# Low parts of the heads' weight tiles: one GpSimd instruction of 1024 columns, or four of 256

## The chip, the cores and the metric

The kernel runs on one core of a Trainium2 chip. A core has five engines that work side by side: TensorE (PE in the profile; PEld is its weight load), VectorE (DVE), ScalarE (ACT), GpSimd (POOL) and SyncE (SP), which issues most transfers. They meet only at semaphores. The metric is device microseconds (us) of the whole program; of several runs the median counts.

## What is computed

One inference step of a decoder layer for 1024 prompt tokens and 8 sample tokens (1032 columns in all), cut to what matters:

```python
xn = rmsnorm(x, p['rms_mix_g']) * (1.0 + sc_m) + sh_m
qa, ka, va, qb, fb, ib, ogb, ga, gb = split_in(xn @ p['w_in'])   # 1024 x (9 * 1024)
oa = attend(rope(rmsnorm(qa)), rope(rmsnorm(ka)), va, lam)       # 8 heads, causal, two softmaxes
ob = recur(silu(qb), 1 - f, log(f), ib)                          # 8 heads, f from sigmoid(fb)
merged = sigmoid(ga) * (oa @ w_branch_a) + sigmoid(gb) * (ob @ w_branch_b)
x = x + g_m * (merged @ p['w_out'])
u = hn @ p['w_up']                                               # then conv, silu(a) * g, @ w_down
```

All of it is in float32.

## The kernel before

**Products in three terms.** Each float32 operand is held as two parts: a high part (`hi`, written by ScalarE in the type fp32r, which TensorE reads) and a low part (`lo` = raw − hi). A product is three matmuls for each of the 8 row blocks `k` of a 1024-row weight tile: hi·hi, hi weights on the low part of x, low weights on the high part of x (`product`, L172). A weight tile is 128x1024: `raw` is loaded by SyncE, `hi` is a ScalarE copy (L780), and `lo` is a subtraction on GpSimd (`lo_of`, L1203), 58 times in the heads stage.

**Stages.** The stages follow one another with a barrier between them: norm (to about 64 us), heads (to about 1092 us), gates, and the tail with the output projections and the feed-forward part. The change lies in the heads stage.

**The heads stage** is a loop over 8 heads. In head `h` TensorE computes 21 *pieces*: 7 weight tiles (`TILES`: f, qh, ib, og of this head, and q, k, v of the next) by 3 column groups of 344. Piece `n` uses tile `n // 3`, so tile 4 (q of the next head) is first used in piece 12, the `FILL_PIECE`. Pieces 0 to 11 lie between the steps of the attention (scores L1072, transposes L1133, values L1110), piece 12 after the transposes of ib (L1078), and pieces 13 to 20 between the steps of the recurrence (products L1151 to L1161, outputs L1186 to L1190). The order of every engine is written out by hand.

**When a weight tile is split.** `SPLIT_AT` says behind which piece number each tile is split, in the order 1, 6, 2, 3, 4, 5, 7 (7 is tile 0 of the next head): tile 4 is split at piece 10, tile 5 at piece 12. ScalarE writes `hi` there and raises `hi_done`; GpSimd waits for it, computes `lo` and raises `lo_done` (one step for a tile). Before the first piece of a tile TensorE waits for both (L1043, L1044):

```python
if j == 0:
    pe.wait_ge(hi_done.sem, hi_done.at(h, SPLIT_ORDER[t]))
    pe.wait_ge(lo_done.sem, lo_done.at(h, SPLIT_ORDER[t]))
```

SyncE waits for `lo_done` too, before it loads the next raw tile into the same buffer (L718).

**GpSimd's other work** in the heads stage, in its one queue: differences for the decays of the recurrence (`differences`, L1234 and L1235, ten short instructions one behind the other without a wait), a rotary product (L1275), low parts of squares (L1241, L1244) and small copies (L1220).

**VectorE's work beside it**, as far as the prediction names it: the cut of a sigmoid's exponential (L1396), the product with a finished sigmoid (L1411), the scan that sums the log decays (L1418), the scale and sum of the two softmaxes (L1388, L1390), the maxima (L1375 to L1379), the masked sums of the recurrence (L1436 to L1443) and its operands (L1427, L1428).

Of the kernel before, what the change touches and what calls it, by code (L numbers as in the profile page):

```python
# [24 lines left out]
F32 = mybir.dt.float32  # L25
# [3 lines left out]
ALU = mybir.AluOpType  # L29
# [3 lines left out]
P = 128  # L33
# [6 lines left out]
KT = D // P  # L40
# [467 lines left out]
RAW_TURN = (0, 1, 2, 2, 3, 3, 1, 4)  # L508
RAW_BEFORE = {6: 0, 2: 1, 3: 6, 4: 2, 5: 3, NTL + 1: 4, NTL: 5, NTL + 2: NTL}
HIGH_AT = (4, 5)  # L510
SQUARES_AT = 6
SUMS_AT, SUMS_BEHIND = 7, 3

# [22 lines left out]
def heads_stage(nc, a, o, c, d, xh, xl, early, banks, gate):  # L536
    with Stage(c) as ctx:
        mem, raw, whi, wlo = early["mem"], early["raw"], early["hi"], early["lo"]
# [63 lines left out]
        def S(n, per, **k):  # L602
            return Sig(ctx, nc, f"h_{n}", per=per, **k)

        loaded = [S("w_loaded0", 4, pre=3, step=16), S("w_loaded1", 3, pre=1, step=16)]
        hi_done, lo_done = S("w_hi_done", 7, pre=4), S("w_lo_done", 7, pre=4)
# [166 lines left out]
        def _(act):  # L773
# [125 lines left out]
            def o_square(h, u):  # L899

                src = oraw if u < 2 else braw
                act.activation(square_high(h, u), src[:, half(u)], ACT.Square).then_inc(o_high.sem, 1)
# [9 lines left out]
            for h in range(H):  # L912
# [58 lines left out]
                for k in range(NB):  # L971
# [12 lines left out]
                    if k == 1 and no_next(h):  # L984
                        act.wait_ge(rows_turned.sem, 1)
                        act.activation(rows[:, :, :], X[0:H * NS, 0, 0:2 * P].rearrange("p (a b) -> p a b", a=2), ACT.Copy).then_inc(rows_ready.sem, 1)
                    if k in HIGH_AT:
                        act.wait_ge(pv_read.sem, pv_read.at(h, NB))
                        o_square(h, HIGH_AT.index(k))
                    if k == SUMS_AT:  # L990
# [207 lines left out]
        def _(pool):  # L1198
# [1 line left out]
            ch = Chain(ctx, nc, pool, "h_pool_chain")  # L1200

            def lo_of(w, r):
                pool.tensor_tensor(wlo[w][:, :], raw[r][:, :], whi[w][:, :].bitcast(F32), ALU.subtract).then_inc(lo_done.sem, 1)  # L1203

            pool.sem_inc(lo_done.sem, 3)
            pool.wait_ge(loaded[0].sem, 16 * 3)
            pool.wait_ge(hi_done.sem, 4)
            lo_of(0, 0)
            sample_rec.start(pool)

            def split_next(h, n):
                if n in SPLIT_AT:
                    t = SPLIT_AT[n]
                    raw_loaded(pool, h, t)
                    pool.wait_ge(hi_done.sem, hi_done.at(h, SPLIT_ORDER[t]))
                    used_wait(pool, h, t)
                    lo_of(slot(t % NTL), RAW_OF[t])
# [34 lines left out]
            for h in range(H):  # L1252
# [16 lines left out]
                for k in range(NB):  # L1269
# [6 lines left out]
                    if k == 0:  # L1276
# [5 lines left out]
                        pool.sem_inc(sample_rec.sem, 1)  # L1282
                    if k == SQUARES_AT:
                        pool.wait_ge(pv_read.sem, pv_read.at(h, NB))
# [10 lines left out]
            pool.wait_ge(hi_done.sem, hi_done.at(H, 1))  # L1295
            used_wait(pool, H, 1)
            lo_of(slot(1), 1)

        @block.vector
# [1572 lines left out]
```

## Time and profile before

| | |
|---|---|
| median of 3 runs | 2310.03 us (2308.55 to 2314.59) |
| time of the profiled execution | 2309.12 us |
| its span, first to last instruction | 2307.3 us |
| TensorE busy | 2270.7 us, 98% |
| VectorE, ScalarE, GpSimd busy | 1438.6, 1065.7, 845.3 us |

The span is the stretch that the trace covers; the time of a run is 1.8 us more. A busy time is the union of an engine's instructions; matmuls overlap, so a wait shorter than a matmul's tail does not show as idle time of TensorE.

### The profile page before, as it was taken

Reading aid. Unit: us, or ns where it says so; the run is one execution under the profiler, and the core shown is the slowest. Engines: PE = TensorE matmul, PEld = TensorE weight load, DVE = VectorE, ACT = ScalarE, POOL = GpSimd, SP = SyncE. Lnnn points to the kernel's source line nnn. Section 1 sums busy time; section 2 is a strip of 40 time slices with the busy share of each in tenths; the row PEclk is TensorE's granted clock in tenths of the full one; section 3 lists DMA queues with packets and bytes.
Section 4 is the critical chain, followed back from the end, with each engine's and each line's share of the span. In section 5 each row is a group of like instructions: output and inputs, shape, how many; then the busy total and the mean of one; then the engine's idle time right before and its main releaser. Section 6 shows DMA issues by size and latency. Waiting matters only on the chain. (4 is left out here: it accounts for less than half of the span.)

```text
span 2307.3 us, 46246 instructions
## 1 busy us (share of the span) xinstructions
PE 2270.7 (98%) x18425; PEld 2152.5 (93%) x18425; DVE 1438.6 (62%) x2595; ACT 1065.7 (46%) x2146; POOL 845.3 (37%) x1051
## 2 busy tenths in 40 slices
PE   7999999999999999999998999999999999999999
PEld 5899999989899999999887999999999999999999
DVE  5667686777777676765887334337545545554556
ACT  6666666666666666654423320135333332332331
POOL 1144352626354444535443125442323322222222
PEclk9999999999999999999999999999999999999999
DMA  7213121221312221311999322121111111111113
GB/s 299 91 50 103 41 90 56 79 71 57 102 57 94 60 93 53 103 43 49 350 343 353 126 88 78 47 62 37 46 46 47 46 46 48 54 46 46 47 47 99
DMA packets 75057, 213.20 MB, mean 92 GB/s; under 512 B 15578, under 2 KB 23642, under 8 KB 74842
## 3 DMA queue, kind: packets, MB, share of 16 engines
q1 hardware_dynamic: 73690, 206.05, 26.8%
q10 hardware_dynamic: 1152, 4.19, 0.4%
q8 instruction: 146, 2.39, 0.4%
q14 instruction: 69, 0.57, 0.1%
HBM read 175.49 MB, written 26.26 MB: 87 GB/s over the span
## 5 line engine op out<-in xcount | busy, mean ns | idle before, releaser
L172 PE MATMUL h_G<-xn_hi,h_w_hi 128*128 128x344 f32 x1368 | 457.3, 334 | 0.2 <-ACT h_d_oraw L918 0.2
L172 PE MATMUL h_G<-xn_hi,h_w_lo 128*128 128x344 f32 x1368 | 437.0, 319 | 0.0
L172 PE MATMUL h_G<-xn_lo,h_w_hi 128*128 128x344 f32 x1368 | 436.6, 319 | 0.0
L2462 POOL TENSOR_TENSOR h_w_lo<-h_w_raw,h_w_hi 128x1024 fp32r<-128x1024 f32 x87 | 215.5, 2477 | 488.8 <-DVE f_y L2663 204.3
L2384 PE MATMUL t_ps<-hn_hi,h_w_hi 128*128 128x344 f32 x1024 | 327.7, 320 | 0.9 <-issue 0.9
L2384 PE MATMUL t_ps<-hn_lo,h_w_hi 128*128 128x344 f32 x1024 | 327.1, 319 | 0.0
L2384 PE MATMUL t_ps<-hn_hi,h_w_lo 128*128 128x344 f32 x1024 | 327.0, 319 | 0.0
L172 PEld LDWEIGHTS h_G<-xn_hi,h_w_hi 128*128 128x128 f32 x1368 | 258.3, 189 | 32.6 <-issue 21.2
L1203 POOL TENSOR_TENSOR h_w_lo<-h_w_raw,h_w_hi 128x1024 fp32r<-128x1024 f32 x58 | 149.3, 2574 | 367.6 <-ACT h_w_hi L780 331.9
L172 PEld LDWEIGHTS h_G<-xn_lo,h_w_hi 128*128 128x128 f32 x1368 | 257.1, 188 | 4.6
L172 PEld LDWEIGHTS h_G<-xn_hi,h_w_lo 128*128 128x128 f32 x1368 | 257.0, 188 | 0.0
L2242 ACT ACTIVATE f_u<-t_ps 128x344 f32<-128x344 f32 x132 | 59.9, 459 | 336.5 <-PE t_ps L2384 335.5
L2192 ACT ACTIVATE h_w_hi<-h_w_raw 128x1024 fp32r<-128x1024 f32 x87 | 91.5, 1052 | 266.5 <-PE t_ps L172 256.8
L2384 PEld LDWEIGHTS t_ps<-hn_hi,h_w_hi 128*128 128x128 f32 x1024 | 192.3, 188 | 1.4 <-issue 1.4
L2384 PEld LDWEIGHTS t_ps<-hn_hi,h_w_lo 128*128 128x128 f32 x1024 | 192.5, 188 | 0.0
L2384 PEld LDWEIGHTS t_ps<-hn_lo,h_w_hi 128*128 128x128 f32 x1024 | 192.3, 188 | 0.0
L2548 DVE SCALAR_TENSOR_TENSOR x<-t_ps,keep_mod,x 128x344 f32<-128x344 f32 (+1 forms) x288 | 149.5, 564 | 68.1 <-PE t_ps L172 67.3
L2656 DVE TENSOR_SCALAR f_y<-f_old,keep_vec 128x8 f32<-128x8 f32 x44 | 16.2, 368 | 259.8 <-ACT f_u L2242 259.8
L172 PE MATMUL t_ps<-f_act_hi,h_w_hi 128*128 128x344 f32 x528 | 169.9, 322 | 0.0
L172 PE MATMUL t_ps<-f_act_hi,h_w_lo 128*128 128x344 f32 x528 | 169.0, 320 | 0.0
L172 PE MATMUL t_ps<-f_act_lo,h_w_hi 128*128 128x344 f32 x528 | 168.7, 320 | 0.0
L1234 POOL TENSOR_TENSOR h_b_level_diff<-h_b_braw 128x64 f32<-128x64 f32 x320 | 97.2, 304 | 137.9 <-ACT h_S L897 115.8
(413 smaller groups left out, 5565.5 us busy)
## 6 DMA issues: line engine op xcount, KB each, us to landing
h_w_raw<-in_w_in SPq DMA_DIRECT2D x72, 512.0 KB, 3.7
h_w_raw<-in_w_ffn SPq DMA_DIRECT2D x66, 512.0 KB, 3.6
h_d_ada_w<-in_w_ada SPq DMA_DIRECT2D x32, 512.0 KB, 4.2
g_kp<-in_cache_k SPq DMA_DIRECT2D x32, 512.0 KB, 6.9
g_vp<-in_cache_v SPq DMA_DIRECT2D x32, 512.0 KB, 5.5
h_w_raw<-in_w_mix SPq DMA_DIRECT2D x24, 512.0 KB, 3.6
x<-in_xT SPq DMA_DIRECT2D x16, 516.0 KB, 7.1
n_ada_w<-in_w_ada SPq DMA_DIRECT2D x16, 512.0 KB, 13.4
```

What stands on the lines that cost most here:

```text
L172: ins = eng.matmul(out, w[:, k * P:(k + 1) * P], x[:, k, columns], start=(k == 0 and n == 0), stop=(k == n_k - 1 and n == 2))
L1203: pool.tensor_tensor(wlo[w][:, :], raw[r][:, :], whi[w][:, :].bitcast(F32), ALU.subtract).then_inc(lo_done.sem, 1)
L1234: ch(pool.tensor_tensor(w[:, :, 0, :], v[:, :, 0, :], mid, ALU.subtract))
L2192: act.activation(whi[buf(n)][:, :], raw[n % 2][:, :], ACT.Copy).then_inc(w_hi.sem, 1)
L2242: act.activation(u[s][:, 2 + j * TH:2 + (j + 1) * TH], ffn_bank(t, 0, j), ACT.Copy).then_inc(up_free.sem, 1)
L2384: ins = pe.matmul(ffn_bank(t, 0, j), wp[w][:, k * P:(k + 1) * P], xp[:, k, cols(j)], start=(k == 0 and q == 0), stop=(k == KT - 1 and q == 2))
L2462: pool.tensor_tensor(wlo[buf(n)][:, :], raw[n % 2][:, :], whi[buf(n)][:, :].bitcast(F32), ALU.subtract).then_inc(w_lo.sem, 1)
L2548: ins = dve.scalar_tensor_tensor(out=xt[:, a0:a0 + n], in0=bank[:, 0:n], scalar=gain[:, 0:1], in1=xt[:, a0:a0 + n], op0=ALU.mult, op1=ALU.add)
L2656: ch(dve.tensor_scalar(ys[:, T:NT], st[0], w[0], w[3], ALU.mult, ALU.add))
```

## The change

`lo_of` cuts the 1024 columns of a weight tile into `LOW_PARTS = 4` slices of 256 and subtracts each in an instruction of its own. All four are issued one behind the other without a wait; the last one alone raises `lo_done`, so TensorE and SyncE still wait for the whole tile. ScalarE's copy, the transfers, all waits and the order of everything else stay. It holds for the 58 tiles of the heads stage; the low parts of the norm, gates and tail stages have code of their own and stay as they are.

```diff
+LOW_PARTS = 4
 ...
             def lo_of(w, r):
-                pool.tensor_tensor(wlo[w][:, :], raw[r][:, :], whi[w][:, :].bitcast(F32), ALU.subtract).then_inc(lo_done.sem, 1)
+
+                for n in range(LOW_PARTS):
+                    s = slice(n * KT * P // LOW_PARTS, (n + 1) * KT * P // LOW_PARTS)
+                    ins = pool.tensor_tensor(wlo[w][:, s], raw[r][:, s], whi[w][:, s].bitcast(F32), ALU.subtract)
+                ins.then_inc(lo_done.sem, 1)
```

GpSimd's queue in the attention of the first head, before: tiles 1, 6, 2 and 3, and behind them the first differences (a row is one instruction or several alike; the names are those of the tiles in memory).

```order
L1203 TENSOR_TENSOR h_w_lo_81<-h_w_raw_77,h_w_hi_79 128x1024
L1203 TENSOR_TENSOR h_w_lo_83<-h_w_raw_76,h_w_hi_82 128x1024
L1203 TENSOR_TENSOR h_w_lo_80<-h_w_raw_77,h_w_hi_78 128x1024
L1203 TENSOR_TENSOR h_w_lo_81<-h_w_raw_76,h_w_hi_79 128x1024
L1234 TENSOR_TENSOR h_b_level_diff<-h_b_braw 128x32x2
```

The same place of the changed kernel:

```order
L1207 TENSOR_TENSOR h_w_lo_81<-h_w_raw_77,h_w_hi_79 128x256 x4
L1207 TENSOR_TENSOR h_w_lo_83<-h_w_raw_76,h_w_hi_82 128x256 x4
L1207 TENSOR_TENSOR h_w_lo_80<-h_w_raw_77,h_w_hi_78 128x256 x4
L1207 TENSOR_TENSOR h_w_lo_81<-h_w_raw_76,h_w_hi_79 128x256 x4
L1239 TENSOR_TENSOR h_b_level_diff<-h_b_braw 128x32x2
```

Each instruction has become four at the same place; nothing stands before or behind anything else than it did.

A little further on, between the first and the second differences, stands tile 4, with the semaphores that an instruction waits for. Before:

```order
L1235 TENSOR_TENSOR h_b_level_diff<-h_b_braw 128x2x32
L1203 TENSOR_TENSOR h_w_lo_80<-h_w_raw_77,h_w_hi_78 128x1024 [waits h_pool_chain,h_piece_done,h_w_hi_done,h_w_loaded1]
L1234 TENSOR_TENSOR h_b_level_diff<-h_b_braw 128x32x2 [waits h_lv_exp]
L1235 TENSOR_TENSOR h_b_level_diff<-h_b_braw 128x32x2
L1234 TENSOR_TENSOR h_b_level_diff<-h_b_braw 128x16x4
```

And in the changed kernel:

```order
L1240 TENSOR_TENSOR h_b_level_diff<-h_b_braw 128x2x32
L1207 TENSOR_TENSOR h_w_lo_80<-h_w_raw_77,h_w_hi_78 128x256 [waits h_pool_chain,h_piece_done,h_w_hi_done,h_w_loaded1]
L1207 TENSOR_TENSOR h_w_lo_80<-h_w_raw_77,h_w_hi_78 128x256 x3
L1239 TENSOR_TENSOR h_b_level_diff<-h_b_braw 128x32x2 [waits h_lv_exp]
L1240 TENSOR_TENSOR h_b_level_diff<-h_b_braw 128x32x2
```

The first slice carries the waits, the other three have none.

## Rows read from the trace of the kernel before

**Rows 1.** The page: span, engines, granted clock in 40 slices.

```profile
span 2307.3 us, 46246 instructions
...
PE 2270.7 (98%) x18425; PEld 2152.5 (93%) x18425; DVE 1438.6 (62%) x2595; ACT 1065.7 (46%) x2146; POOL 845.3 (37%) x1051
...
PEclk9999999999999999999999999999999999999999
```

**Rows 2.** Heads stage: busy PE, PEld, DVE, ACT, POOL; clock; DMA share; GB/s.

```profile
64.00:1092.00 1028.00, 1024.44 (x10313) 937.32 (x10311) 736.69 (x1369) 646.69 (x1599) 447.58 (x868) 1.00 0.23 72
```

**Rows 3.** Waits of PE, heads stage: total us, times, longest us.

```profile
PE h_X L172 <- DVE keep_ones_r L179: 0.9, 1, 0.9
```

**Rows 4.** The page, costliest groups: count, busy us, mean ns of one.

```profile
L172 PE MATMUL h_G<-xn_hi,h_w_hi 128*128 128x344 f32 x1368 | 457.3, 334 | 0.2 <-ACT h_d_oraw L918 0.2
L172 PE MATMUL h_G<-xn_hi,h_w_lo 128*128 128x344 f32 x1368 | 437.0, 319 | 0.0
```

**Rows 5.** Line L1203: count, ns min/median/max, first and last start.

```profile
L1203 POOL TENSOR_TENSOR h_w_lo<-h_w_raw,h_w_hi x58: 2358/2540/2960, 69.7 to 1084.1; 128x1024 fp32r<-128x1024 f32 x58
```

**Rows 6.** Timeline of the third head about piece 12: start us, length us, instruction.

```profile
396.78 0.51 DVE L1411 TENSOR_TENSOR h_og<-h_og,h_b_ex 128x344 f32<-128x344 f32 x1
...
396.91 2.61 POOL L1203 TENSOR_TENSOR h_w_lo<-h_w_raw,h_w_hi 128x1024 fp32r<-128x1024 f32 x1 [17.03 <-ACT h_w_hi L780]
...
398.29 1.43 DVE L1396 TENSOR_SCALAR h_b_ex<-h_b_ex 128x344 f32<-128x344 f32 x1 [1.00 <-ACT h_b_ex L847]
...
399.64 0.51 DVE L1411 TENSOR_TENSOR h_og<-h_og,h_b_ex 128x344 f32<-128x344 f32 x1
...
399.78 0.39 PE L172 MATMUL h_G<-xn_hi,h_w_hi 128*128 128x344 f32 x1
...
400.01 0.31 PE L172 MATMUL h_G<-xn_lo,h_w_hi 128*128 128x344 f32 x1
```

**Rows 7.** Line L1044, 399 to 400 us: count, ns, first and last start.

```profile
L1044 PEldq EVENT_SEMAPHORE  x1: 51/51/51, 399.6 to 399.6; - x1
```

**Rows 8.** Timeline of the eighth head about piece 12.

```profile
1022.21 2.61 POOL L1203 TENSOR_TENSOR h_w_lo<-h_w_raw,h_w_hi 128x1024 fp32r<-128x1024 f32 x1 [17.03 <-ACT h_w_hi L780]
...
1025.08 0.39 PE L172 MATMUL h_G<-xn_hi,h_w_hi 128*128 128x344 f32 x1
```

**Rows 9.** Timeline of the third head, tile 2.

```profile
360.19 2.96 POOL L1203 TENSOR_TENSOR h_w_lo<-h_w_raw,h_w_hi 128x1024 fp32r<-128x1024 f32 x1 [11.33 <-ACT h_w_hi L780]
...
361.33 2.00 DVE L1396 TENSOR_SCALAR h_b_ex<-h_b_ex 128x344 f32<-128x344 f32 x1 [0.45 <-ACT h_b_ex L847]
...
365.81 0.42 PE L172 MATMUL h_G<-xn_hi,h_w_hi 128*128 128x344 f32 x1
```

**Rows 10.** Lines of GpSimd: 64 and 344 columns; count, ns min/median/max.

```profile
L1234 POOL TENSOR_TENSOR h_b_level_diff<-h_b_braw x320: 284/295/410, 127.9 to 1064.7; 128x64 f32<-128x64 f32 x160
...
L1275 POOL TENSOR_TENSOR h_d_rg<-h_d_rg,h_cos x42: 907/920/1123, 161.3 to 942.8; 128x344 f32<-128x344 f32 x42
```

**Rows 11.** Timeline of GpSimd: two instructions without a wait between.

```profile
323.88 1.28 POOL L1244 TENSOR_TENSOR h_rstd_osq_low<-h_d_rstd_o,h_vtok_osq_high 128x512 fp32r<-128x512 f32 x1
325.12 2.40 POOL L1203 TENSOR_TENSOR h_w_lo<-h_w_raw,h_w_hi 128x1024 fp32r<-128x1024 f32 x1
```

**Rows 12.** Line L1396: count, ns min/median/max.

```profile
L1396 DVE TENSOR_SCALAR h_b_ex<-h_b_ex x72: 326/340/2005, 87.8 to 1023.6; 128x344 f32<-128x344 f32 x72
```

**Rows 13.** Timeline of the third head, start of the recurrence.

```profile
405.71 2.38 POOL L1203 TENSOR_TENSOR h_w_lo<-h_w_raw,h_w_hi 128x1024 fp32r<-128x1024 f32 x1 [0.27 <-POOL h_b_level_diff L1235]
...
408.53 0.29 DVE L1440 TENSOR_TENSOR h_AT<-h_spot_near_sum,h_spot_same_mask 128x128 f32<-128x128 f32 x1
408.57 0.40 POOL L1234 TENSOR_TENSOR h_b_level_diff<-h_b_braw 128x64 f32<-128x64 f32 x1 [0.48 <-ACT h_S L897]
```

**Rows 14.** Timeline of the third head, PE at the third chunk.

```profile
417.53 0.39 PE L1190 MATMUL h_S<-h_ibtok,h_kht 128*128 128x128 f32 x2
418.06 0.27 PE L1151 MATMUL h_S<-h_fc,h_kk 128*32 128x32 f32 x8
```

## The prediction

> **What bounds the kernel.** I read the page first: TensorE is busy for 98% of the span, the next engine for 62%, and the granted clock stands at its highest digit in all 40 slices, so it is at 2.4 GHz before and will be after [rows 1]. Then the stretch of the heads stage, since only that stage changes: in 1028 us TensorE is idle for 3.6 us [rows 2], and its longest wait that shows as idle time is 0.9 us, at the stage's start [rows 3]. So what the change saves on GpSimd (447.6 us busy of 1028, [rows 2]) or VectorE is worth nothing by itself; the time moves by what reaches TensorE. But matmuls overlap, and a wait of a tenth of a microsecond hides in a tail: the first of the three matmuls of a row block lasts 334 ns in the mean, the others 319 [rows 4]. 15 ns for 1368 of them is 20.5 us, and this is all that TensorE can still be waiting for inside its pieces. The question is where it waits for `lo_done`, so I went through the timeline tile by tile and compared the end of each L1203 with the first matmul of the tile's first piece.
>
> Tile 4 is the one that counts. Its subtraction runs from 396.91 to 399.52, and piece 12 begins at 399.78 [rows 6]; the wait instruction for `lo_done` (L1044) goes through at 399.6, right behind the subtraction's end [rows 7]. The first matmul lasts 0.39 us instead of 0.32 and the second begins 0.23 us behind it, where two others stand about 0.16 apart (319 ns each, overlapping by half): some 0.07 us are lost to this wait already. It is no accident of one head: the eighth has 1022.21 + 2.61 = 1024.82 and a start at 1025.08, again 0.26 [rows 8], and all eight heads have 0.26 to 0.29. The tile with the next smallest margin is tile 2, whose subtraction ends at 363.15 with its piece at 365.81, 2.66 us later [rows 9]; all the others have over 5 us.
>
> So a longer subtraction of tile 4 delays TensorE in each of the 8 heads, one for one. TensorE waits for nothing else for long behind it, and the other engines' work behind piece 12 starts from TensorE's results, so nothing gives the delay back.
>
> **The price of four instructions for one.** GpSimd's subtraction takes 1.28 us for 512 columns [rows 11], 0.92 for 344 [rows 10] and 2.38 for 1024 when nothing disturbs it [rows 13]. That is (2.38 - 1.28) / 512 = 2.15 ns a column, and 1.28 - 512 x 2.15 / 1000 = 0.18 us fixed; 344 columns then make 0.92, as seen. 256 columns make 0.55 + 0.18 = 0.73 us. Two instructions without a wait between them overlap a little: 323.88 + 1.28 = 325.16, and the next begins at 325.12 [rows 11]. So three slices at 0.69 and a last of 0.73 are 2.80 us, **0.42 us** more than 2.38.
>
> The Trainium skill (Perfetto Trace Analysis, GPSIMD Engine Instruction) says that a GpSimd instruction's span in a profile is unreliable and that consecutive ones should be timed from start to start. Four full spans, 4 x 0.73 - 2.38, would make 0.54 us instead of 0.42, and 1.0 us more over eight heads; the 0.04 of overlap in the row agrees with the rule in kind.
>
> **What VectorE does in the cracks.** The two engines block each other. The cut L1396 takes 0.34 us as a rule and 2.00 at worst [rows 12]: that one starts at 361.33, inside tile 2's subtraction, and ends at 363.33, 0.18 behind the subtraction's end at 363.15 [rows 9]. For tile 4 it starts at 398.29 and ends at 399.72, 0.20 behind 399.52 [rows 6]. The other way round the subtraction of tile 4, which starts 0.13 us behind an L1411, takes 2.61 instead of 2.38, so an L1411 shuts GpSimd out for 0.13 + 0.23 = 0.36 us from its start. The Trainium skill (SBUF — State Buffer, SBUF: two separate sides) calls this an exclusive lock that is held for the whole instruction, with TensorE and ScalarE outside of it; the rows above agree.
>
> With slices the lock falls free three times. Does VectorE get it there? Short back-to-back instructions answer that: at 408.53 an L1440 starts just ahead of the first L1234, is not held up (0.29) and stretches that one to 0.40 [rows 13], where the median is 0.295 [rows 10]. I take it that a waiting VectorE instruction gets in at the next boundary. Then, from the 397.14 at which the first slice really gets going, slices end near 397.87, 398.56, 399.25 and 399.94. L1396 asks at 398.29 and gets in at 398.56, for 0.18. The L1411 behind it, today at 399.64, follows and takes 0.36 before the last slice. Sum 0.54; as the row of L1234 shows 0.11 for an instruction that should have held about 0.13, part of it is hidden behind the fixed part of a slice, and I take **0.50**. The bounds are 0, if GpSimd's four keep VectorE out, and 0.62, if nothing is hidden and each of the two turns also costs the 0.04 of overlap.
>
> **The sum.** 0.42 + 0.50 = 0.92 us for a tile 4, less perhaps 0.02 of rounding in the margin, 0.90; eight heads make **7.2 us**. The profiled execution took 2309.12 (span 2307.3 and 1.8 around it), so it would take 2316.3; the median of the runs shown is 0.9 above it, so I forecast **2317.2 us**, 0.31% slower. What a measurement of this kernel tells from no change is about 0.3%, 6.9 us: the forecast lies on that line.
>
> Edits that cost nothing: of the 58 subtractions, today 2.54 us in the median [rows 5], the other 50 grow by 0.42 to about 1.0 us too. Tile 2's 2.66 us of margin cover that, and if they were gone each microsecond beyond would cost 8. Tile 5's runs from 405.71 to 408.09, and the differences behind it wait another 0.48 us for ScalarE [rows 13]: 0.42 just fits, and since tile 5 does not start from TensorE's work while the rest does, the new delay of piece 12 widens the room. SyncE's next loads start later by as much; ScalarE splits what they bring in much later, so nothing waits for them.
>
> **Rivals.**
> - *Only the fixed cost.* The four slices hold the lock among them, or VectorE's turns hide behind their fixed parts: 8 x 0.42 = 3.4 us, 2313.4. For it: the slices overlap by 0.04, so GpSimd asks again before it has let go. Against it: L1440 above. Chance 0.20.
> - *No price at all.* TensorE's queue still holds transposes when L1044 goes through, and if the wait isn't what delays piece 12, or a slice's fixed part runs in the shadow of the one before: 2310, within 1.5 us. Against it: the same 0.26 in eight heads. Chance 0.14.
> - *Faster, the other side: relief of VectorE.* Slices give VectorE back up to 1.66 us in one place (2.00 against 0.34). If a chain through VectorE ends in a hidden wait of TensorE, this is earned there. A place is the recurrence's third chunk: between the last outputs at 417.53 and the products at 418.06 lie 0.53 us [rows 14]; with all of it gone, 8 x 0.53 = 4.2 us, less than tile 4's price. To decide the sign it must give back more than the 0.90 us a head of tile 4, and to be measured as faster 1.8 us a head; the 20.5 us of [rows 4] are the ceiling, at 2.6 us a head. If three quarters of the 20.5 came back, 15 us, less the 7.2, the time would be 2302. Against it: VectorE's L1396 and L1411 there end microseconds before TensorE needs their tiles. Chance 0.05.
> - *More than that.* VectorE gets a turn of L1411's length in each of the three cracks: 0.42 + 3 x 0.36 = 1.50 us, 12 us in all, 2322. Against it: only two of its instructions stand there to ask. Chance 0.08.
> - *The forecast.* Both turns taken: 5.5 to 9 us. Chance 0.53.
>
> **How the numbers follow.** The forecast's own case lies above 6.9 us about two times in three, 0.35; with the last rival slower is 0.43. Faster is 0.05. The rest, 0.52, is no measurable change. The range from 2309.5 to 2321 takes in the forecast's case, the fixed cost alone and most of "no price", and leaves the two outer rivals out.
>
> **What would show it.** In the trace after: L1207 of 256 columns at about 0.73 us, started every 0.69; L1396 beside tile 4 at 0.45 to 0.6 us instead of 1.43; tile 4 taking from its first start to its last end 3.4 to 3.6 us; piece 12 still 0.26 behind that end, and the distance between the starts of one piece in successive heads longer by 0.9 than today's 125.1 (1025.08 - 399.78 is 625.30 for five heads). Tail and gates unchanged. The prediction is wrong if piece 12 starts at its old place in the head though the slices end later, or if the heads grow by something other than piece 12's start.

## The result and the profile after

| | before | after |
|---|---|---|
| median of 17 runs each | 2309.57 us (2305.71 to 2314.59) | 2316.47 us (2313.58 to 2320.26) |
| ratio after / before | | 1.0029, 95% interval 1.0023 to 1.0036 |
| span of the profiled execution | 2307.3 us | 2315.5 us |

The changed kernel is 6.9 us slower, 0.29%: a loss that 17 runs tell from zero, and one that lies on the 0.3% that the prediction had set as its line. (The ratio is an estimate of its own; it differs a little from the quotient of the two medians, here and in the table of the experiments.) These rows of the changed kernel's page stand beside [rows 1] and [rows 4]. In a costly group the columns are count, busy us, mean ns of one, and idle time of the engine ahead of it with what ended it:

```profile
span 2315.5 us, 46420 instructions
...
PE 2274.5 (98%) x18425; PEld 2155.2 (93%) x18425; DVE 1425.2 (62%) x2595; ACT 1067.1 (46%) x2146; POOL 881.5 (38%) x1225
...
PEclk9999999999999999999999999999999999999999
...
L172 PE MATMUL h_G<-xn_hi,h_w_hi 128*128 128x344 f32 x1368 | 457.9, 335 | 5.2 <-POOL h_w_lo L1207 5.0
...
L1207 POOL TENSOR_TENSOR h_w_lo<-h_w_raw,h_w_hi 128x256 fp32r<-128x256 f32 x232 | 185.7, 830 | 354.7 <-issue 179.1
```

The granted clock stands at its highest digit throughout, as before, so it has no part in the loss. VectorE is busy for 13.4 us less, GpSimd for 36.2 us more, and a wait of TensorE for the low parts has appeared where [rows 4] had 0.2 us in all. In the list of TensorE's waits (total us, times, longest us) it has a line of its own, with eight waits, one in each head:

```profile
PE h_G L172 <- POOL h_w_lo L1207: 5.0, 8, 0.6
```

These 5.0 us are the idle time that shows; the start of piece 12, read below, gives the full delay.

The timeline of the third head, the place of [rows 6] (start us, length us; the four slices of a tile are merged into one row, since they have no gap):

```profile
399.29 0.51 DVE L1416 TENSOR_TENSOR h_og<-h_og,h_b_ex 128x344 f32<-128x344 f32 x1
...
399.43 3.39 POOL L1207 TENSOR_TENSOR h_w_lo<-h_w_raw,h_w_hi 128x256 fp32r<-128x256 f32 x4 [17.20 <-ACT h_w_hi L781]
...
400.80 0.47 DVE L1401 TENSOR_SCALAR h_b_ex<-h_b_ex 128x344 f32<-128x344 f32 x1 [1.00 <-ACT h_b_ex L848]
...
401.19 1.04 DVE L1416 TENSOR_TENSOR h_og<-h_og,h_b_ex 128x344 f32<-128x344 f32 x1
...
403.07 0.40 PE L172 MATMUL h_G<-xn_hi,h_w_hi 128*128 128x344 f32 x1 [0.61 <-POOL h_w_lo L1207]
```

Tile 4's low part takes 3.39 us instead of 2.61, and piece 12 starts 0.25 us behind its end (0.26 before). A yardstick that can be read in every kernel of this study, the *run-up*, is the stretch from the start of VectorE's product ahead of the tile (the first row; L1411 in [rows 6]) to the first matmul of piece 12: 399.78 - 396.78 = 3.00 us before, 403.07 - 399.29 = 3.78 now. It has grown by 0.78. The same line asked for one slice at a time (count, ns min/median/max, first and last start) shows where:

```profile
L1207 POOL TENSOR_TENSOR h_w_lo<-h_w_raw,h_w_hi x1: 966/966/966, 399.4 to 399.4; 128x256 fp32r<-128x256 f32 x1
...
L1207 POOL TENSOR_TENSOR h_w_lo<-h_w_raw,h_w_hi x1: 724/724/724, 400.4 to 400.4; 128x256 fp32r<-128x256 f32 x1
...
L1207 POOL TENSOR_TENSOR h_w_lo<-h_w_raw,h_w_hi x1: 819/819/819, 401.0 to 401.0; 128x256 fp32r<-128x256 f32 x1
...
L1207 POOL TENSOR_TENSOR h_w_lo<-h_w_raw,h_w_hi x1: 995/995/995, 401.8 to 401.8; 128x256 fp32r<-128x256 f32 x1
```

The second slice is undisturbed. The first carries the 0.23 us that it already had before, from the product in front of it. The third is 0.09 us longer than 0.73: VectorE's cut L1401 stood between it and the second. The fourth is 0.27 us longer: the product L1416 stood there. What four slices cost without a neighbour stands in tile 5, where VectorE leaves them alone (timeline, and the line asked for that stretch; [rows 13] had 2.38):

```profile
408.21 2.81 POOL L1207 TENSOR_TENSOR h_w_lo<-h_w_raw,h_w_hi 128x256 fp32r<-128x256 f32 x4 [0.27 <-POOL h_b_level_diff L1240]
```

```profile
L1207 POOL TENSOR_TENSOR h_w_lo<-h_w_raw,h_w_hi x4: 729/732/733, 408.2 to 410.3; 128x256 fp32r<-128x256 f32 x4
```

So 0.42 us are the instructions themselves (2.81 against 2.38, less rounding), and 0.09 + 0.27 = 0.36 are VectorE's. Over eight heads that makes 8 x 0.78 = 6.2 us. The eighth head has piece 12 at this row:

```profile
1032.70 0.39 PE L172 MATMUL h_G<-xn_hi,h_w_hi 128*128 128x344 f32 x1 [0.62 <-POOL h_w_lo L1207]
```

(1032.70 - 403.07) / 5 = 125.93 us a head against 125.06 before, 0.87 more. Of the 21 distances between successive pieces only that from piece 11 to 12 has grown in every head; the other 0.4 us of the five heads lie in single places (0.2 of them between pieces 14 and 15 of one head) and are left unexplained.

Tile 2, whose margin was the next smallest, takes 3.75 us instead of 2.96:

```profile
362.70 3.75 POOL L1207 TENSOR_TENSOR h_w_lo<-h_w_raw,h_w_hi 128x256 fp32r<-128x256 f32 x4 [10.73 <-issue]
...
363.86 0.34 DVE L1401 TENSOR_SCALAR h_b_ex<-h_b_ex 128x344 f32<-128x344 f32 x1 [0.45 <-ACT h_b_ex L848]
...
368.32 0.42 PE L172 MATMUL h_G<-xn_hi,h_w_hi 128*128 128x344 f32 x1
```

Its piece starts 1.87 us behind its end, so nobody waits. Beside it VectorE's cut takes 0.34 us where [rows 9] had 2.00; the longest L1401 of the whole kernel is 0.66 us (2.005 in [rows 12]):

```profile
L1401 DVE TENSOR_SCALAR h_b_ex<-h_b_ex x72: 325/340/664, 88.8 to 1030.4; 128x344 f32<-128x344 f32 x72
```

### The profile page after: what moved, and what is told of

Same layout as the page of the kernel before. It is cut to its first block and busy times, and to the rows that moved or that the text cites. A ratio compares the mean times of both kernels' runs of the same rounds, so it can differ in the third digit from the quotient of the medians.

```text
span 2315.5 us, 46420 instructions
## 1 busy us (share of the span) xinstructions
PE 2274.5 (98%) x18425; PEld 2155.2 (93%) x18425; DVE 1425.2 (62%) x2595; ACT 1067.1 (46%) x2146; POOL 881.5 (38%) x1225
## 5 line engine op out<-in xcount | busy, mean ns | idle before, releaser
L2467 POOL TENSOR_TENSOR h_w_lo<-h_w_raw,h_w_hi 128x1024 fp32r<-128x1024 f32 x87 | 215.3, 2475 | 489.9 <-DVE f_y L2668 208.9
L1207 POOL TENSOR_TENSOR h_w_lo<-h_w_raw,h_w_hi 128x256 fp32r<-128x256 f32 x232 | 185.7, 830 | 354.7 <-issue 179.1
L929 ACT ACTIVATE h_a_E<-h_S,h_d_sm 128x256 f32<-128x256 f32 (+7 forms) x128 | 93.5, 738 | 120.0 <-DVE h_d_sm L1384 120.0
```

What stands on the lines that cost most here:

```text
L929: ins = act.activation(E[:, m, 0:nk], SP_[:, :, :].rearrange("p a b -> p (a b)")[:, 512 * score_bank(i, m):512 * score_bank(i, m) + nk], A ...
L1207: ins = pool.tensor_tensor(wlo[w][:, s], raw[r][:, s], whi[w][:, s].bitcast(F32), ALU.subtract)
L2467: pool.tensor_tensor(wlo[buf(n)][:, :], raw[n % 2][:, :], whi[buf(n)][:, :].bitcast(F32), ALU.subtract).then_inc(w_lo.sem, 1)
```

## The experiments

The theory: only tile 4's low part is on TensorE's path; its length grows by a fixed cost for each further instruction and by what VectorE takes at the boundaries, and TensorE waits until the last slice. Rivals: the loss comes from another tile, or from GpSimd's queue as a whole; the length is fixed cost alone; VectorE's relief gives part of it back. "Tile 4" is the time from the start of its first subtraction to the end of its last, "run-up" the yardstick above, both in the third head. Each set of four was run together with the kernel before, which had a median of 2309.66 us beside the first four rows and 2309.01 us beside the last four. Line numbers of the kernels differ by a few.

| kernel | median us | ratio to before, 95% | tile 4, us | run-up, us |
|---|---|---|---|---|
| tile4_whole | 2310.39 | 0.9999 (0.9990 to 1.0008) | 2.61 | 2.99 |
| tile4_alone | 2316.93 | 1.0026 (1.0015 to 1.0037) | 3.40 | 3.79 |
| two_parts | 2311.93 | 1.0008 (0.9999 to 1.0017) | 2.85 | 3.24 |
| early_four | 2310.38 | 1.0003 (0.9994 to 1.0012) | 3.86 | 2.92 |
| vector_kept_out | 2312.99 | 1.0019 (1.0010 to 1.0028) | 3.03 | 3.42 |
| eight_parts | 2319.86 | 1.0047 (1.0034 to 1.0061) | 3.97 | 4.36 |
| early_whole | 2309.32 | 0.9999 (0.9990 to 1.0008) | 2.98 | 2.92 |
| signal_each | 2309.42 | 1.0002 (0.9993 to 1.0011) | 3.41 | 2.93 |

**Which tile? tile4_whole and tile4_alone.** The first leaves tile 4 in one instruction and slices the other 50; the second slices tile 4 alone.

```diff
-            def lo_of(w, r):
+            def lo_of(w, r, parts=LOW_PARTS):
...
-                    lo_of(slot(t % NTL), RAW_OF[t])
+                    lo_of(slot(t % NTL), RAW_OF[t], 1 if t == 4 else LOW_PARTS)
```

In tile4_alone the default is `parts=1` and the call passes `LOW_PARTS if t == 4 else 1`; in both, `parts` stands in the loop where `LOW_PARTS` stood.

> Every weight tile of the heads stage in four slices but tile 4, which is one instruction of 1024 columns again. Theory A (the whole loss is the later lo_done of tile 4, 0.8 us in each of 8 heads): 0 to +0.5 us against the kernel before, ratio 1.000; piece 12 starts 0.26 us behind a subtraction of 2.61 us, and one head follows the other at 125.1 us. Theory B (the slices of the other 50 tiles, or VectorE's changed turns among them, cost something too): the part of the 6.9 us that is theirs stays, for all of it ratio 1.003.

> Only tile 4 of each head in four slices, the other 50 tiles in one instruction as before. Theory A: +6.4 to +6.9 us, ratio 1.0028, tile 4 at 3.4 us, heads 125.9 us apart. Theory B: clearly less than +6.9 us, for all of it ratio 1.000.

With tile 4 whole the loss is gone and the timeline is that of [rows 6] again:

```profile
399.41 0.51 DVE L1416 TENSOR_TENSOR h_og<-h_og,h_b_ex 128x344 f32<-128x344 f32 x1
...
399.54 2.61 POOL L1207 TENSOR_TENSOR h_w_lo<-h_w_raw,h_w_hi 128x1024 fp32r<-128x1024 f32 x1 [17.20 <-ACT h_w_hi L781]
...
400.92 1.43 DVE L1401 TENSOR_SCALAR h_b_ex<-h_b_ex 128x344 f32<-128x344 f32 x1 [1.00 <-ACT h_b_ex L848]
...
402.40 0.40 PE L172 MATMUL h_G<-xn_hi,h_w_hi 128*128 128x344 f32 x1
```

With tile 4 sliced alone all of it is back; its line among TensorE's waits:

```profile
PE h_G L172 <- POOL h_w_lo L1207: 5.0, 8, 0.7
```

Eight of the 58 tiles carry the whole loss, as far as these runs can tell. The other 50, with their longer subtractions and with the relief that they give VectorE, are worth between -0.1% and +0.08% together, so no measurable part is earned back.

**How the length grows: two_parts and eight_parts.** Only the constant differs.

```diff
-LOW_PARTS = 4
+LOW_PARTS = 2        # eight_parts: 8
```

> Two slices of 512 columns for every tile. Fixed cost of one more instruction 0.14 us, and one crack in tile 4, at which one VectorE instruction (the cut, 0.15 to 0.2) gets a turn while the product behind it must wait for the end: 2.61 + 0.14 + 0.17 = 2.9 us for tile 4, 8 x 0.3 = +2.4 us, ratio 1.0010. If the loss were only the fixed cost: 8 x 0.14 = +1.1 us, ratio 1.0005. If it were the same whatever the size: +6.9 us.

> Eight slices of 128 columns. Fixed cost 7 x 0.14 = 0.98 us against one instruction, turns of VectorE 0.3 to 0.5 as with four: tile 4 at 3.9 to 4.1 us, +1.3 to 1.5 us a head, +10 to +12 us in all, ratio 1.0048. If the price did not grow with the number of slices: +6.6 us, ratio 1.0029. Tile 2's margin would be about 1.2 us, still enough.

Tile 5, undisturbed, in two and in eight parts (timelines):

```profile
408.80 2.51 POOL L1207 TENSOR_TENSOR h_w_lo<-h_w_raw,h_w_hi 128x512 fp32r<-128x512 f32 x2 [0.27 <-POOL h_b_level_diff L1240]
```

```profile
411.27 3.36 POOL L1207 TENSOR_TENSOR h_w_lo<-h_w_raw,h_w_hi 128x128 fp32r<-128x128 f32 x8 [0.27 <-POOL h_b_level_diff L1240]
```

2.38, 2.51, 2.80 and 3.36 us for 1, 2, 4 and 8 instructions: 0.14 us for each further one. Tile 4 in two parts, where VectorE's product comes too late to get in:

```profile
400.00 2.85 POOL L1207 TENSOR_TENSOR h_w_lo<-h_w_raw,h_w_hi 128x512 fp32r<-128x512 f32 x2 [17.09 <-ACT h_w_hi L781]
...
401.38 0.34 DVE L1401 TENSOR_SCALAR h_b_ex<-h_b_ex 128x344 f32<-128x344 f32 x1 [1.00 <-ACT h_b_ex L848]
...
401.63 1.59 DVE L1416 TENSOR_TENSOR h_og<-h_og,h_b_ex 128x344 f32<-128x344 f32 x1
...
403.11 0.40 PE L172 MATMUL h_G<-xn_hi,h_w_hi 128*128 128x344 f32 x1
```

The cut starts inside the first half and is through behind the boundary; the product then stays shut out until the tile is done (403.22, behind 402.85). So tile 4 grows by 0.14 + 0.09, and 2.85 - 2.61 = 0.24 were measured. The time alone shows only that the loss is smaller than with four: its interval, -0.2 to +3.9 us, holds both the 1.9 us of 8 x 0.24 and the 1.1 us of the fixed cost alone, and it is the trace that tells them apart. In eight parts both get in, at the earliest boundary that suits them:

```profile
402.47 3.97 POOL L1207 TENSOR_TENSOR h_w_lo<-h_w_raw,h_w_hi 128x128 fp32r<-128x128 f32 x8 [17.43 <-ACT h_w_hi L781]
...
403.85 0.35 DVE L1401 TENSOR_SCALAR h_b_ex<-h_b_ex 128x344 f32<-128x344 f32 x1 [1.00 <-ACT h_b_ex L848]
...
404.12 0.77 DVE L1416 TENSOR_TENSOR h_og<-h_og,h_b_ex 128x344 f32<-128x344 f32 x1
```

Worked out are 0.98 + 0.09 + 0.27 = 1.34 us, measured 3.97 - 2.61 = 1.36; eight heads make 10.9 us, and the median of the 5 runs is 10.9 above that of before. VectorE's share does not grow with the number of boundaries: there are only two instructions to let in.

**VectorE's share taken away: vector_kept_out.** VectorE waits for tile 4's low part before the cut, so that it does not ask at a boundary.

```diff
                             s = SIGMOID.index(n)
+                            if s == 8:
+                                dve.wait_ge(lo_done.sem, lo_done.at(h, SPLIT_ORDER[4]))
```

> The changed kernel, and VectorE's cut of the last sigmoid (which today gets its turn behind the second slice of tile 4), and with it the product behind it, wait for lo_done of tile 4. So nothing of VectorE stands in the cracks of tile 4. If the 0.79 us are 0.42 fixed and 0.37 for two turns of VectorE, tile 4 takes 2.61 + 0.42 = 3.03 us and the time is +3.4 us, ratio 1.0015. If the turns cost nothing and the slices are dearer there for another reason: +6.5 us, ratio 1.0028.

```profile
398.65 0.51 DVE L1416 TENSOR_TENSOR h_og<-h_og,h_b_ex 128x344 f32<-128x344 f32 x1
...
398.78 3.03 POOL L1207 TENSOR_TENSOR h_w_lo<-h_w_raw,h_w_hi 128x256 fp32r<-128x256 f32 x4 [17.20 <-ACT h_w_hi L781]
...
401.85 0.34 DVE L1401 TENSOR_SCALAR h_b_ex<-h_b_ex 128x344 f32<-128x344 f32 x1 [2.69 <-POOL h_w_lo L1207]
...
402.07 0.39 PE L172 MATMUL h_G<-xn_hi,h_w_hi 128*128 128x344 f32 x1 [0.25 <-POOL h_w_lo L1207]
```

Tile 4 takes 3.03 - 2.61 = 0.42 us more than before: the fixed cost and nothing else. The run-up falls from 3.78 to 3.42, the 0.36 that VectorE had taken. The median is 4.0 us above that of before, where 3.4 were expected and 6.5 if the turns cost nothing; the interval, 2.3 to 6.5 us, just reaches the second, so here too the trace decides. Of the changed kernel's loss a little over half is the fixed cost, the rest the two turns. VectorE starts its cut 3.20 us behind its product here (398.65 to 401.85), 1.7 us later than in the changed kernel (1.51), and the run-up is no longer for it: a second sign that its relief is worth nothing.

**The wait taken away: early_four and early_whole.** Tile 4 is split one piece earlier, at piece 9, in both; early_four keeps the four slices, early_whole has one instruction a tile (`LOW_PARTS = 1`). ScalarE's copy of tile 4 moves too, so early_whole is also the check on what the move itself costs.

```diff
-SPLIT_AT = {1: 1, 2: 6, 4: 2, 7: 3, 10: 4, 12: 5, 19: 7}
+SPLIT_AT = {1: 1, 2: 6, 4: 2, 7: 3, 9: 4, 12: 5, 19: 7}
```

> The changed kernel (four slices everywhere), but tile 4 is split at piece 9 instead of piece 10, so its low part is ready some 7 to 10 us earlier. Theory A: TensorE no longer waits there, the slices cost nothing, the time is that of the kernel before or 0.5 us less (the 0.07 us a head that were lost already): ratio 0.9997 to 1.0000, unless ScalarE's copy in the new place delays a step of the attention. Theory B: +6.9 us stay, ratio 1.003.

> The kernel before (one instruction for a tile), but tile 4 is split at piece 9 instead of piece 10. Piece 12 no longer waits: 0.08 us a head less, -0.6 us, ratio 0.9997, too little to be told from no change by the time, but seen in the distance from piece 11 to piece 12 (7.01 us instead of 7.09). If ScalarE's copy at its new place were in the way: more than 7.09.

Tile 4 of early_four, which ends at 387.99 for a piece that starts at 400.42 (timeline; the last row is piece 12):

```profile
384.13 3.86 POOL L1207 TENSOR_TENSOR h_w_lo<-h_w_raw,h_w_hi 128x256 fp32r<-128x256 f32 x4 [3.70 <-ACT h_w_hi L781]
...
397.50 0.51 DVE L1416 TENSOR_TENSOR h_og<-h_og,h_b_ex 128x344 f32<-128x344 f32 x1
...
400.42 0.40 PE L172 MATMUL h_G<-xn_hi,h_w_hi 128*128 128x344 f32 x1
```

Four slices that take even longer (3.86 us) cost nothing when they end 12.4 us before the piece that needs them. Both kernels have a run-up of 2.92, 0.08 less than before: that is what the old kernel was already losing at this wait, where its profile showed no idle time. Eight times 0.08 are 0.6 us, too little for the runs to show (0.9999, 0.9990 to 1.0008), so early_whole is no version to prefer on this evidence.

**The last slice's signal: signal_each.** The place and the four slices stay; each slice of tile 4 raises a semaphore, and TensorE waits before row blocks 0, 2, 4 and 6 for the slice that it is about to use.

```diff
+            def part_wait(h, k):
+                if k in (2, 4):
+                    pe.wait_ge(lo_part.sem, lo_part.at(h, 1 + k // 2))
+                elif k == 6:
+                    pe.wait_ge(lo_done.sem, lo_done.at(h, SPLIT_ORDER[4]))
...
+                    if n == FILL_PIECE and h < H:
+                        pe.wait_ge(lo_part.sem, lo_part.at(h, 1))
...
+                    if each and n < LOW_PARTS - 1:
+                        ins.then_inc(lo_part.sem, 1)
```

> The changed kernel with split at piece 10 as before, but for tile 4 each slice raises a semaphore of its own, and TensorE waits for slice n only before row block 2n of piece 12. The first slice is done about 1 us behind the start, the fourth about 0.8 us later than the one instruction was, when TensorE is in its second row block. Theory A: nothing is lost, -0.6 to +0.5 us, ratio 1.000, and piece 12 begins before the last slice ends. If the slices cost TensorE something other than the wait for the last of them: +6.6 us stay.

```profile
397.33 0.51 DVE L1430 TENSOR_TENSOR h_og<-h_og,h_b_ex 128x344 f32<-128x344 f32 x1
...
397.47 3.41 POOL L1219 TENSOR_TENSOR h_w_lo<-h_w_raw,h_w_hi 128x256 fp32r<-128x256 f32 x4 [17.20 <-ACT h_w_hi L784]
...
400.26 0.40 PE L174 MATMUL h_G<-xn_hi,h_w_hi 128*128 128x344 f32 x1
```

GpSimd is as slow as in the changed kernel (3.41), VectorE takes the same turns, but piece 12 begins at 400.26, 0.62 us before the last slice ends at 400.88. The loss is gone (1.0002, 0.9993 to 1.0011), and so is the old 0.07 of the run-up, which reads 2.93. So the slices delay TensorE only through its wait for the last of them.

## Why the prediction was right

- **The place.** Tile 4 and piece 12, in all eight heads, one for one: shown by tile4_whole and tile4_alone from both sides, and by the two early kernels and signal_each, which take the wait away.
- **The fixed cost, 0.42 us.** It came out as worked out: 2.80 us undisturbed, slices of 0.73, and 0.42 for tile 4 with VectorE kept out. The other sum, full spans of 0.73 one behind the other, would have given 0.54; no row has it.
- **VectorE's turns, 0.50 us.** The mechanism held, the term was too large: measured 0.36. The prediction let the cut cost 0.18 and the product 0.36 and took off 0.04 for what a slice hides; in the trace they cost 0.09 and 0.27. The row of L1234 in [rows 13] (0.11 us of stretch) gave too weak a hint of it. Nor does that row show what the step needs, that a *waiting* VectorE instruction gets in between two of GpSimd: L1440 started at 408.53, before L1234 did at 408.57, and simply came first. The step was an assumption ("I take it"), and it was the runs after the prediction that bore it out.
- **The sum.** 0.90 us a head were predicted, 0.78 measured, 7.2 us against 6.2; the medians lie 6.9 apart. The runs can't tell 6.2 from 6.9 (the interval is 5.3 to 8.3 us), so that the total came closer than the term is chance as far as these runs show. The traces are finer: from the start of piece 0 in the first head to that of piece 20 in the eighth, 989.5 us before, the changed kernel takes 6.7 us more and tile4_alone 6.5, of which the eight starts of piece 12 explain 6.3.
- **The others.** Only the fixed cost (3.4 us) is what vector_kept_out measures, and it lies below the changed kernel's interval. No price is out, since that interval lies clear of zero. A gain by VectorE's relief did not show: in tile4_whole, where 50 tiles still give it, nothing moved beyond 0.1%, though VectorE is busy for 13.4 us less in the changed kernel. A turn in all three cracks is out: the second slice is undisturbed.
- **Edits at nothing.** Tile 2 kept 1.87 of its 2.66 us, and in eight parts still a little under 1. Tile 5 grew by 0.42, and the differences behind it now wait 0.85 us for ScalarE where they had waited 0.48: the later piece 12 did widen the room, as foreseen (timeline):

```profile
411.88 0.40 POOL L1239 TENSOR_TENSOR h_b_level_diff<-h_b_braw 128x64 f32<-128x64 f32 x1 [0.85 <-ACT h_S L898]
```

Of the tests named ahead: slices of 0.73 started every 0.69 (held), the cut at 0.45 to 0.6 (0.47), tile 4 at 3.4 to 3.6 (3.39 to 3.41, the lower edge), piece 12 still 0.26 behind (0.25 to 0.26, held), heads longer by 0.9 (0.87, of which 0.78 at piece 12).

## What to carry to other kernels

Cutting an instruction into slices can help its reader only if each slice tells the reader that it is there; with one signal behind the last, the reader here got the fixed costs and the neighbour's turns on top. Before cutting, find the instances on the path by comparing each instance's end with its first use: here 8 of 58 carried all of the loss, and tile 2, with 2.66 us of margin, took the same edit for free. A price that is certain in its fixed part and uncertain in its contention is best split the way vector_kept_out does it: hold the neighbour back by a wait and read the rest.

## What the runs showed of the hardware

- **GpSimd's price of one more instruction** in a chain without waits was 0.14 us, the same for 2, 4 and 8 slices (2.38, 2.51, 2.80, 3.36 us in 1, 2, 4 and 8 instructions, for 1024 columns of float32 with two inputs).
- **The lock between GpSimd and VectorE changes hands at the boundary of two GpSimd instructions that follow without a gap**, each time that VectorE's cut or product was waiting at tile 4, in all eight heads. The Trainium skill (SBUF — State Buffer, SBUF: two separate sides) has it that whoever starts first holds the shared pair for the whole instruction; that agrees (the product beside the second of two halves ends only at 403.22, behind that half's end at 402.85), and the runs add that a queued GpSimd instruction does not extend the hold.
- **A turn costs less at a boundary than at a start.** The product cost tile 4's first slice 0.36 us from its own start (0.13 until the slice's start and 0.23 of stretch), but 0.27 at a boundary; the cut, held 0.18 to 0.20 us past the lock's release, cost 0.09. That 0.09 us of a slice's fixed part run while the lock is away fits both, but this cause was only argued.
- **A wait of TensorE can cost 0.08 us and show no idle time.** The run-up of 3.00 us fell to 2.92 when tile 4 came early, while the profile before listed no wait for it.
- **Cutting moved work forward where nothing waited for it.** The Trainium skill (Perfetto Trace Analysis, Optimizing Scalar/DVE Operations) says that breaking up instructions may let work be completed sooner when ScalarE or VectorE, though not saturated, cause bubbles on other engines. Here VectorE's work did end sooner (0.34 us instead of 2.00 beside tile 2), but TensorE had no bubble from it, and got one from GpSimd instead.
